# Gated linear attention in a hybrid decoder step: decay levels of two chunks packed into one product

## The reference

```python
b = jnp.cumsum(gc, axis=2)
diff = b[:, :, :, None, :] - b[:, :, None, :, :]
decay = jnp.exp(jnp.where(causal[:, :, None], diff, -jnp.inf))
att = jnp.einsum('bhtd,bhsd,bhtsd->bhts', qc, kc, decay)
o = (jnp.einsum('bhts,bhsv->bhtv', att, vc)
     + jnp.einsum('bhtd,bhdv->bhtv', qc * jnp.exp(b), S))
```

## Time and profile before

| | us |
|---|---|
| median of 3 runs (1196.51 to 1202.24) | 1196.52 |
| the profiled execution | 1196.73 |
| its span, first to last instruction | 1195.0 |
| mean granted TensorE clock, share of full | 0.996 |
| PE busy / DVE busy / ACT busy / POOL busy | 1161.8 / 531.4 / 420.4 / 188.4 |

### The profile page before, as it was taken

The page is one execution under the profiler, slowest core; times in us unless marked ns, Lnnn a source line. Parts: engine busy times, 40 slices in busy tenths (PEclk is TensorE's granted clock), DMA queues, the critical chain, the costliest instruction groups (busy, mean ns, idle before and its releaser), DMA issues.

```text
span 1195.0 us, 18057 instructions
## 1 busy us (share of the span) xinstructions
PE 1161.8 (97%) x7032; PEld 1121.1 (94%) x7032; DVE 531.4 (44%) x667; ACT 420.4 (35%) x549; POOL 188.4 (16%) x101
## 2 busy tenths in 40 slices
PE   5899999999999999999999999999999999999997
PEld 5899999999999999998999999999999999999886
DVE  5777777774000001844465455438434001434332
ACT  6555554444111113433533452454335121122121
POOL 4211111112121211110211011111102121210000
PEclk9999999999999999999999999999989999999999
DMA  6211111111212222100311121031002103442321
GB/s 208 69 52 40 39 39 39 39 36 54 71 54 71 73 72 92 41 19 18 112 35 35 59 70 35 18 111 35 18 18 75 53 18 108 136 133 90 105 105 53
DMA packets 95488, 76.18 MB, mean 64 GB/s; under 512 B 3928, under 2 KB 88792, under 8 KB 95464
## 3 DMA queue, kind: packets, MB, share of 16 engines
q1 hardware_dynamic: 84444, 61.59, 17.4%
q10 hardware_dynamic: 11020, 14.26, 3.5%
HBM read 62.04 MB, written 13.80 MB: 63 GB/s over the span
## 4 chain that ended last, share of the span: by engine, by line
issue 76%; PE 14%; POOL 8%; POOLq 0%; DVE 0%; ACT 0%; DVEq 0%
POOL wlo L437 7%; PE ps L447 5%; PE ps L448 5%; PE ps L449 5%; POOL lmask L420 0%; POOLq L439 0%; POOL lmask L418 0%; DVE yy L1462 0%; DVE yy L1456 0%; ACT junk L1089 0%; POOLq L436 0%; POOL notfirst L429 0%; POOLq L437 0%; POOL lmask L417 0%; POOL smask L424 0%
## 5 line engine op out<-in xcount | busy, mean ns | idle before, releaser
L447 PE MATMUL ps<-xn,whi 128*128 128x364 f32 x1344 | 450.8, 335 | 1.5 <-DVE xn L1106 1.5
L448 PE MATMUL ps<-xn,whi 128*128 128x364 f32 x1344 | 442.3, 329 | 0.0
L449 PE MATMUL ps<-xn,wlo 128*128 128x364 f32 x1344 | 441.8, 329 | 0.0
L437 POOL TENSOR_TENSOR wlo<-raw,whi 128x1024 fp32r<-128x1024 f32 x72 | 179.4, 2492 | 884.6 <-ACT whi L803 884.6
L447 PEld LDWEIGHTS ps<-xn,whi 128*128 128x128 f32 x1344 | 253.2, 188 | 5.7 <-issue 2.5
L448 PEld LDWEIGHTS ps<-xn,whi 128*128 128x128 f32 x1344 | 253.5, 189 | 0.2
L449 PEld LDWEIGHTS ps<-xn,wlo 128*128 128x128 f32 x1344 | 252.9, 188 | 0.0
L803 ACT ACTIVATE whi<-raw 128x1024 fp32r<-128x1024 f32 x72 | 76.0, 1055 | 152.6 <-PE ps L449 85.5
L447 PE MATMUL ps<-act_s,whi 128*128 128x364 f32 x384 | 126.3, 329 | 0.4 <-POOL wlo L437 0.4
L448 PE MATMUL ps<-act_s,whi 128*128 128x364 f32 x384 | 126.2, 329 | 0.0
L449 PE MATMUL ps<-act_s,wlo 128*128 128x364 f32 x384 | 126.1, 328 | 0.0
(11 more groups left out here) (229 smaller groups left out, 1356.7 us busy)
## 6 DMA issues: line engine op xcount, KB each, us to landing
raw<-in_w_in SPq DMA_DIRECT2D x56, 512.0 KB, 3.8
branch_a<-keep ACTq DMA_DIRECT2D x8, 546.0 KB, 2.8
mal<-branch_a SPq DMA_DIRECT2D x8, 544.0 KB, 4.9
xt<-in_x_prompt SPq DMA_DIRECT2D x8, 512.0 KB, 6.8
raw<-in_w_lru_o SPq DMA_DIRECT2D x8, 512.0 KB, 3.6
st<-in_state_gla ACTq DMA_DIRECT2D x4, 1024.0 KB, 5.5
out<-st ACTq DMA_DIRECT2D x4, 1024.0 KB, 4.6
raw<-in_w_gla_o SPq DMA_DIRECT2D x8, 512.0 KB, 5.8
```

The costliest lines, as they stand in the source:

```text
L437: pool.tensor_tensor(wlo[:, c % 2], raw[:, c % 2], whi[:, c % 2].bitcast(F32), ALU.subtract).then_inc(s["lo_ok"], 1)
L447: pe.matmul(dst, wh, mh, start=first, stop=False)
L448: pe.matmul(dst, wh, ml, start=False, stop=False)
L449: return pe.matmul(dst, wl, mh, start=False, stop=last)
```

## The change

- All 7 levels are packed alike. For a pair of chunks 2i and 2i+1, the even tile of `qk` holds the even chunk's keys in its first-half blocks and the odd chunk's queries in its second-half blocks; the odd tile holds the odd chunk's keys and the even chunk's queries. One product of the two tiles gives, in its quadrants, the even chunk's block with keys on partitions and the odd chunk's block with queries on partitions. So each level has four products of 128 x 128, and the odd chunks' part of `att` comes out turned.
- `level_operands` writes three products on DVE (512, 256 and 256 columns) in place of two (512 and 512).
- `keep_level` makes two masked copies of 256 columns each at every level, in place of one of 512 or the plain copies. The masks are bf16 and there are 14 (7 levels, two sides), 64 columns each.
- The odd chunks of `att` are cleared by DVE at the start of each head (4 x 128 columns), between `distance(1)` and the wait for q.
- Two new steps, `att0` and `att1`: PE turns two odd chunks each (`turn`), ACT copies them back to `att`. `turn(0)` stands after `kTc`, `turn(1)` before KV0. NSTEP goes from 38 to 40.
- POOL does the first `lo` ahead of the masks, then all masks, then the second `lo`.
- ACT takes exponentials 5 and 6 ahead of the evacuation of job 3.

```diff
-            for l, m in enumerate(LEVELS[PACKED:]):
-                mask = lmask[:, l, :]
-                step(pool.memset(mask, 1.0))
-                step(pool.affine_select(out=mask, in_=mask, compare_op=ALU.is_ge, fill=0.0, base=0,
-                                        pattern=[[-2 * m, 64 // m], [0, m]], channel_multiplier=1))
-                step(pool.affine_select(out=mask, in_=mask, compare_op=ALU.is_ge, fill=0.0, base=m - 1,
-                                        pattern=[[2 * m, 64 // m], [0, m]], channel_multiplier=-1))
+            lo(0, 0)
+            for l, m in enumerate(LEVELS):
+                for w in range(2):
+                    mask = lmask[:, l, w, :]
+                    step(pool.memset(mask, 1.0))
+                    step(pool.affine_select(out=mask, in_=mask, compare_op=ALU.is_ge, fill=0.0, base=-w * m,
+                                            pattern=[[-2 * m, 64 // m], [0, m]], channel_multiplier=1))
+                    step(pool.affine_select(out=mask, in_=mask, compare_op=ALU.is_ge, fill=0.0, base=(w + 1) * m - 1,
+                                            pattern=[[2 * m, 64 // m], [0, m]], channel_multiplier=-1))
...
-            with pool.Fori(0, (N_YB + KT) // 2) as i:
+            lo(0, 1)
+            with pool.Fori(1, (N_YB + KT) // 2) as i:
...
                     def emit(b):
-                        if l < PACKED:
-                            for c in range(0, SEQ // 2, P):
-                                ins = pe.matmul(ps[:, b, c:c + P], qk[:, l % 2, c:c + P], qk[:, l % 2, SEQ // 2 + c:SEQ // 2 + c + P],
-                                                start=True, stop=True)
-                            return ins
-                        for c in range(NCHUNK):
-                            tile = qk[:, l % 2, c * P:(c + 1) * P]
-                            ins = pe.matmul(ps[:, b, c * 64:(c + 1) * 64], tile, half(tile, LEVELS[l], 1), start=True, stop=True)
+                        for i in range(PAIRS):
+                            ins = pe.matmul(ps[:, b, i * P:(i + 1) * P], qk[:, l % 2, 2 * i * P:(2 * i + 1) * P],
+                                            qk[:, l % 2, (2 * i + 1) * P:(2 * i + 2) * P], start=True, stop=True)
                         return ins
                     c_step(f"L{l}", emit)
+
+                def turn(n):
+                    def emit(b):
+                        for i in range(2):
+                            ins = pe.transpose(ps[:, b, i * P:(i + 1) * P], att[:, 4 * n + 2 * i + 1, :], ident[:, :])
+                        return ins
+                    c_step(f"att{n}", emit)
...
                 transposes("kT", kt, "bc")
+                pe.wait_ge(*emptied(h, "L6"))
+                turn(0)
                 part(5, bankB, 1, EARLY)
+                turn(1)
                 pe.wait_ge(*emptied(h, "kTc"))
                 outer(0)
...
+                    pe.wait_ge(*emptied(h, "att1"))
                     pe.wait_ge(*emptied(h, f"KV{2 * g + 1}"))
...
                 token_tiles("vt0", value0, "bc")
+                level_exp(5)
+                level_exp(6)
                 job_at(3)
                 act.activation(p3(vT[:, :]), slot3(bankB), ACT.Copy).then_inc(s["vT_ok"], 1)
                 hi(3 * h, N_GLA + 5)
-                level_exp(5)
-                level_exp(6)
...
                 token_tiles("kT", key, "abc")
+                for n in range(2):
+                    full(f"att{n}")
+                    act.activation(att[:, 4 * n + 1:4 * n + 4:2, :], ps[:, bank(f"att{n}"), 0:2 * P].rearrange("p (c n) -> p c n", n=P),
+                                   ACT.Copy).then_inc(s["c_act"], 1)
...
-                    dve.tensor_tensor(dsts[0], half(kb[:, 0:SEQ], m, 0), half(src[:, 0:SEQ], m, 0), ALU.mult)
-                    dve.tensor_tensor(dsts[1], half(qb[:, 0:SEQ], m, 1), half(src[:, 0:SEQ], m, 1), ALU.mult).then_inc(s["lev_qk"], 1)
+                    dve.tensor_tensor(half(qk[:, l % 2, 0:SEQ], m, 0), half(kb[:, 0:SEQ], m, 0), half(src[:, 0:SEQ], m, 0), ALU.mult)
+                    for w in range(2):
+                        ins = dve.tensor_tensor(second_halves(qk[:, l % 2, 0:SEQ], m, 1 - w), second_halves(qb[:, 0:SEQ], m, w),
+                                                second_halves(src[:, 0:SEQ], m, w), ALU.mult)
+                    ins.then_inc(s["lev_qk"], 1)
...
-                    dst = att[:, 0:NCHUNK, :].rearrange("p c (q h m) -> p c q h m", h=2, m=m)[:, :, :, 1, :]
-                    mask = lmask[:, l - PACKED, :].bitcast(U32).rearrange("p (o q m) -> p o q m", o=1, m=m).to_broadcast([P, NCHUNK, 64 // m, m])
-                    dve.copy_predicated(dst, mask, ps[:, bank(f"L{l}"), :].rearrange("p (c q m) -> p c q m", c=NCHUNK, m=m)).then_inc(s["c_dve"], 1)
+                    for w in range(2):
+                        dst = att[:, w:NCHUNK:2, :].rearrange("p i (q h m) -> p i q h m", h=2, m=m)[:, :, :, 1 - w, :]
+                        mask = lmask[:, l, w, :].bitcast(U16).rearrange("p (o q m) -> p o q m", o=1, m=m).to_broadcast([P, PAIRS, 64 // m, m])
+                        src = ps[:, bank(f"L{l}"), :].rearrange("p (i q h m) -> p i q h m", i=PAIRS, h=2, m=m)[:, :, :, 1 - w, :]
+                        ins = dve.copy_predicated(dst, mask, src)
+                    ins.then_inc(s["c_dve"], 1)
...
                 distance(0)
                 distance(1)
+                dve.memset(att[:, 1:NCHUNK:2, :], 0.0).then_inc(s["att_zero"], 1)
```

More of the change, by code:

```diff
@@ L32 @@
 U32 = mybir.dt.uint32
+U16 = mybir.dt.uint16
 ALU = mybir.AluOpType
@@ L56 @@
 LEVELS = (64, 32, 16, 8, 4, 2, 1)
-PACKED = 2
+PAIRS = NCHUNK // 2
 SLEVELS = (4, 2, 1)
@@ L96, in head_steps @@
     steps += [("vt1a", "act"), ("vt1b", "act"), ("vt1c", "act"), ("smp", "dve")]
-    steps += [("kTa", "act"), ("kTb", "act"), ("kTc", "act")]
+    steps += [("kTa", "act"), ("kTb", "act"), ("kTc", "act"), ("att0", "act"), ("att1", "act")]
     steps += [(f"KV{n}", "dve") for n in range(NCHUNK // 2)]
@@ L142, in build @@
         notfirst = take("notfirst", [P, TOK], BF16, TOK * 2)
-        lmask = take("lmask", [P, len(LEVELS) - PACKED, 64], F32, (len(LEVELS) - PACKED) * 64 * 4)
+        lmask = take("lmask", [P, len(LEVELS), 2, 64], BF16, len(LEVELS) * 2 * 64 * 2)
         smask = take("smask", [P, NSEQ], F32, NSEQ * 4)
@@ L307, in half, with second_halves @@
             return ap.rearrange("p (n h m) -> p n h m", h=2, m=m)[:, :, which, :]
+        def second_halves(ap, m, w):
+            return ap.rearrange("p (i w n h m) -> p i w n h m", i=PAIRS, w=2, h=2, m=m)[:, :, w, :, 1, :]
         y_rows = [(out[0][0], n * P, P) for n in range(NCHUNK)] + [(out[1].rearrange("a b d -> (a b) d"), 0, STOK)]
@@ L1286, in keep_level @@
                     order(f"L{l}")
-                    if l < PACKED:
-                        blocks = P // m
-                        for n in range(blocks):
-                            c, q = n * 2 // blocks, n % (blocks // 2)
-                            ins = dve.tensor_copy(att[2 * m * q:2 * m * q + m, c:NCHUNK:2, 2 * m * q + m:2 * m * (q + 1)],
-                                                  ps[n * m:(n + 1) * m, bank(f"L{l}"), :].rearrange("p (c t) -> p c t", t=P)[:, :, n * m:(n + 1) * m])
-                        ins.then_inc(s["c_dve"], 1)
-                        return
-                    dst = att[:, 0:NCHUNK, :].rearrange("p c (q h m) -> p c q h m", h=2, m=m)[:, :, :, 1, :]
-                    mask = lmask[:, l - PACKED, :].bitcast(U32).rearrange("p (o q m) -> p o q m", o=1, m=m).to_broadcast([P, NCHUNK, 64 // m, m])
-                    dve.copy_predicated(dst, mask, ps[:, bank(f"L{l}"), :].rearrange("p (c q m) -> p c q m", c=NCHUNK, m=m)).then_inc(s["c_dve"], 1)
+                    for w in range(2):
[4 more added lines that the diff above has]
+                    ins.then_inc(s["c_dve"], 1)
                 def keep_diagonal(n):
@@ L1321, in _ @@
                 distance(2)
+                dve.wait_ge(s["att_zero"], h + 2)
                 keep_diagonal(0)
@@ L1342, in _ @@
                 for l, m in enumerate(SLEVELS):
-                    mask = lmask[0:STOK, LEVELS.index(m) - PACKED, 0:32].bitcast(U32).rearrange("p (q m) -> p q m", m=m)
+                    mask = lmask[0:STOK, LEVELS.index(m), 0, 0:32].bitcast(U16).rearrange("p (q m) -> p q m", m=m)
                     dve.copy_predicated(half(att[0:STOK, NCHUNK, 0:STOK], m, 1), mask,
```

6 lines of the change are left out of this document (3 added, 3 removed).

## The result

| | before | after |
|---|---|---|
| median of 4 runs each, us | 1199.38 (1196.51 to 1203.22) | 1182.69 (1181.49 to 1186.15) |
| ratio, 95% interval | | 0.9864 [0.9834, 0.9894] |
| profiled run / its span, us | 1196.73 / 1195.0 | 1186.15 / 1184.4 |

Measured again in two more sets, the changed kernel stood at 0.9883 [0.9861, 0.9904] and 0.9902 [0.9873, 0.9931]. The three ratios lie around 0.988, which is 14 us; the forecast of -12.3 us is 0.990. To read the profiles one must know that both kernels show stretches with a lower granted clock, at the start and in the tails of heads, and how many of these an execution has differs: one run of the changed kernel took 1182.56 us at a mean clock of 0.995 and another 1188.37 at 0.986. So I take the change's price from heads that no such stretch touches, and come to the clock last.

A forecast was written before the change was run, and what follows sets the result against it. PE, busy for 97% of the span, was taken as the bound. The terms -17.8 - 2.1 + 5.6 + 0.6 + 1.4 = -12.3 us took 1196.7 to 1184.4 us, range 1179 to 1191.

The forecast's parts named there:

- The forecast case: Whole kernel: the summed terms hold, around 1184.4 us; chance 0.70.
- levels and level 5's stop: PE: four products replace eight in 20 levels, 17.8 us less; level 5's stop goes in four heads, 2.1 us less.
- turns: PE after `kTc`: turns cost 1.5 us, and waiting for ACT's copy of `kTb` 4.1; 5.6 us in all.
- `vt0b`: Bank shared with level 2: whether PE stops for DVE's masked pair is a toss; half a restart, 0.6 us in all.
- start: POOL's 14 masks make the second split 2.6 us late; the `xcs` idle time absorbs 1.24, cost 1.4 us once.
- with a restart of 0.26 as at level 5: At `turn(0)`: PE idles 0.77 us and the restart adds 0.26, so 1.03 us a head, 4.1 in all.
- the dear end of the range: POOL's masks at the start: 28 selects each 0.99 us longer, 27.7 us, nearly all on PE's path.
- Masks somewhat late: POOL at the start: bf16 selects or contention cost 3 to 8 us more, 1187 to 1192 us; chance 0.12.
- masks that block: Second `lo` behind 28 selects, each 0.99 us longer, ends near 68 us; 1208.1 us, slower; chance 0.03.
- DVE late: Each masked copy of 256 columns costs 1.32 us, stopping `vt0b`; 9.2 us over four heads, 1193.6 us; chance 0.06.
- columns: Levels on PE: 16 instructions of 64 columns cost the same as 8 of 128, no 17.8 us gain; 1202.2 us; chance 0.02.
- The free bank: The turn finds its bank free through PE's order or a faster copy: 4.1 us less, 1180.3 us; chance 0.07.

The follow-up runs named there:

- half the columns: Changed kernel with 64 instead of 128 moving columns in every product of the levels, half of each level's result left out; 1179.63 us, one run.
- the dearer level 2: Changed kernel with one more DVE copy of 512 columns ahead of level 2's masked copies; 1183.7 us, one run.
- both edits: Changed kernel with the first turn early, after `kTa`, and POOL's other constants behind the second split; 1180.96 us (0.9838), again 1182.99 us (0.9883).
- the edit that makes it free: Changed kernel with the first turn (`att0`) moved between `kTa` and `kTb`, amid job 5's first piece; 1184.71 us, ratio 0.9872.

## Why the prediction was right, term by term

The forecast case happened, and the range holds all three medians of the changed kernel (1182.69, 1185.6, 1184.76). That they lie within 2 us of 1184.4 is in part luck. The forecast started from 1196.7, a low value: the medians of the kernel before were 1199.38, 1200.19, 1199.91 and 1198.36 in the four sets, some 3 us more. And the gain was 14 us where it said 12.3. The two errors cancel in the time, not in the gain.

| term | predicted | measured | from |
|---|---|---|---|
| levels and level 5's stop | -19.9 | -19.6 | 4 x (3.47 + 1.43), starts in head 0 |
| level 0 | not in the sum | +0.6 | 4 x 0.15, starts in head 2 |
| turns | +5.6 | +4.9 | 4 x (0.82 + 0.41), starts; 4.9 to 5.0 by the kernel without turns |
| `vt0b` | +0.6 | 0 | starts 0.25 after its bank is free |
| start | +1.4 | +0.4 | 462.03 to 462.06 against 461.66 |
| sum | -12.3 | -13.7 | whole heads and the start: 4 x -3.56 + 0.4 = -13.8 |

**Levels.** By starts in head 0, level 5 with its piece gives 1.43, and levels 2, 3, 4 and 6 give 3.47 a head (0.84 to 0.90 each): 4.9, 19.6 in four. That bears out 0.89 a level and the stop's 0.5. By the isolated formula of the Trainium skill (TensorE: Matmul & The Clock Gate, Back-to-back issue gap) the levels would have gained nothing; in this stream eight instructions took 0.80 us with half the columns, so the trace speaks against using it here. The split into 17.8 and 2.1 hid that the second isn't a fixed sum: the exponentials' move was priced against the old arrival of PE. In the new kernel it carries 6 us, because without it the gain of level 4, 0.9 a head, would be waited away at level 5 on top of the old stop. Levels 2 and 3 keep theirs, since they bring the end of job 3 forward too.

**Level 0.** The prediction had 2.5 us of cover for DVE ahead of level 0's operands, and these came in time (in head 0 DVE wrote them by 491.71, and the level began at 493.68). What it left out is the bank: level 0 takes the one of `dg0`, whose copy stands behind the clearing, the third operand product and the next distance in DVE's order. With 0.5 us of new work ahead of it and PE's turn no later, the copy ends at 710.16 just where PE arrives, and level 0 with its surroundings costs 1.12 instead of 0.97. That is the 0.7 us in the row of the weight loads, in all four heads. No run takes the clearing away, so the cause is read from the order of times and not shown by an edit. By luck it is about what the sum had given to `vt0b`.

**Turns.** The mechanism was as told: `att0` waits for ACT's copy of the bank it shares with `kTb`. PE would have been there at 535.11 + 0.47 = 535.58, the copy ended at 536.35: 0.77 us between, to the hundredth what the step has, and `turn(0)` began 0.05 later. The step that failed is "with a restart of 0.26 as at level 5": there the restart was the difference between a stop and the idle time shown, and that idle time counts from the last product's modelled end, here 535.11 + 0.71 = 535.82 (0.58 before 536.40). Of the 0.26 at level 5, 0.16 is that, and 0.10 the level itself, 1.80 us instead of 1.70 behind the stop. My 0.77 already ran from start to start, so the restart was in it, and I counted it twice. 4 x 0.21 = 0.84 us too much for the stop, less 0.2 too little for the turns (0.41 a head, not 0.36), is the 0.7 by which the term was too dear. The turns cost 0.19 and 0.22, and the second outer step had no stop: 0.82 + 0.41 = 1.23 a head, which is what the kernel without turns gives.

**`vt0b`.** The pair at level 2 took 0.77, not 0.85, and ended 0.25 before PE came. I called it a toss and gave half a restart; the dearer level 2 shows how near the edge is.

**Start.** The mechanism was as told: PE's second job late behind POOL, the idle time for `xcs` absorbed by it. With half the columns the second split ended at 41.38 + 2.36 = 43.74, predicted 44.6; PE was ready at 41.89 + 0.17 = 42.06 and started at 43.79, 1.73 late and not 2.6. Less the 1.24 that is 0.5, and 0.4 by the way to level 0. So the term was too dear because POOL was done 0.9 us sooner than priced. In the first profile it ended at 43.2. From the first split to the second it took 40.80 - 20.02 = 20.8 us instead of 22.1: the masks 0.4 less than priced (0.82 instead of 0.89 for one with blocks of 64), the constants 2.5 instead of 3.0 (from 38.34), and the five scalings held it up by 3.6 us instead of 4.0, as one select behind each took 0.90 to 1.23 us, the one at 20.24 among them. That PE stopped only 0.20 us in that profile is its slowed first job. With both edits the product starts at 55.79 and not at 55.28, with the idle time for `xcs` as before; 0.47 of these 0.51 us are there at 31.51 (before 31.04), a scatter of the first job between executions that reaches 30.86 in the changed kernel. The sentence that putting the first split ahead gains nothing was true of five masks and false of 14: behind them it would cost 4 us.

The Trainium skill (GPSIMD Engine Reference, 1. Specifications) has POOL contend with DVE where DVE reads two SBUF inputs; the trace agrees: each of the five long selects (0.90 to 1.23 us, 1.02 at 20.24) overlaps a scaling, which reads two tiles in SBUF, while the select at 21.33 took 0.25 beside DVE's split of `xn`, which has one of its inputs in PSUM. It was five of 28 that met a scaling, so the dear end of the range was far off.

**The rivals.** Masks somewhat late, masks that block, DVE late and columns: none came, though DVE's copies are the reason at level 0. The free bank came only by the edit that makes it free, and is worth 3 us, not 4.1, since 0.78 a head comes back of the stop's 0.82.

**The clock** was missing from the sum. It moves single executions by more than most terms: 5.8 us in the first profile after. It needs no term in a comparison of medians, but a profile of after against one of before gave -10.6, and in the profiles only undisturbed heads show the 14 behind it.

## What to carry to other kernels

Price a stop where its cause sits, by who arrives when after the whole change, not by the idle time that the old trace shows: speeding up PE by 0.9 us made a 0.5 us stop into one of 1.5. Where a kernel repeats a head or a tile, measure an edit from the start of one repetition to the next in stretches of like clock; that resolved 0.07 us where twelve timed runs could not see 2. When a step is put into a ring of banks, look up whose copy it waits for: moving it two steps forward gave back 0.8 of its 1.2 us.

## What the runs showed that I had not expected

- The granted clock falls to its lower level in the tail of a head, where PE is busy and runs its 8-column products (0.51 at 560 to 566 us), and at the start, behind PE's waits for the activation tiles (0.67 at 20 to 30). It does so in some executions and not in others with the same instructions, in the kernel before too, and costs up to 4.4 us a head. What decides it no run shows.
- An fp32 product in the stream, two instructions, takes 0.20 us with 64 moving columns as with 128 (0.80 and 0.81 for four).
- PE's row can show no idle time where its weight loads waited: level 0 became 0.15 us dearer in each head, at 0.0 of idle time for PE and 0.7 for PEld.
- A masked copy depends on the length of its runs: 2 x 256 columns take 0.77 to 0.78 us at levels 0 to 4 (runs of 64 to 4) and 1.31 at levels 5 and 6 (runs of 2 and 1). One instruction of 512 columns does the same, 0.70 to 0.73 and 1.32.
- POOL's selects of 64 columns take 0.24 us in blocks of 16 and more and up to 0.66 in blocks of 1, and 0.5 to 1.0 us more when DVE scales a tile beside them (0.8 at 20.24).
